# Ten gated pieces rounded by ScalarE in one go at the end of banded attention, with the step tables of the last two tiles written anew

## The reference, cut to what matters

```python
logits = einsum("bnqkgd,bnskd->bnkgqs", q, k_band) + bias      # window of 128 keys
m = maximum(max(logits), sink); p = exp(logits - m)
probs = p / (sum(p) + exp(sink - m))
o = einsum("bnkgqs,bnskd->bnqkgd", probs, v_band)
o = o.reshape(B, T, 2048) * silu(z)
x = x + o @ w_out                                              # b_w_out: 2048 x 1024
```

## Time and profile before

| | |
|---|---|
| median of 3 runs | 1502.39 us (1501.16 to 1502.45) |
| the profiled execution | 1503.07 us, of it a span of 1501.2 us |
| PE busy | 1480.6 us, 99% of the span |
| DVE, ACT, POOL busy | 926.2, 736.8, 259.7 us |
| mean granted TensorE clock | 0.998 of full speed |
| chain that ended last | PE 90%, DVE 5%, ACT 3% |

### The profile page before, as it was taken

One profiled execution on the slowest core, in us unless ns is written; L12 is line 12 of the kernel. 1 busy time (PEld: TensorE's weight loads), 2 busy tenths in 40 slices (PEclk: granted clock), 3 DMA queues, 4 the chain that ended last, 5 costly groups with the idle time before them and its releaser, 6 DMA issues.

```text
span 1501.2 us, 20571 instructions
## 1 busy us (share of the span) xinstructions
PE 1480.6 (99%) x7595; PEld 1185.0 (79%) x7595; DVE 926.2 (62%) x1740; ACT 736.8 (49%) x1292; POOL 259.7 (17%) x430
## 2 busy tenths in 40 slices
PE   9999999999999999999998999999999999999998
PEld 7878888888778878888877887665778888888887
DVE  5867777787655468788886346554475243433467
ACT  5454455644553356566675234665465241423343
POOL 1034323344302015444440000000000000000000
PEclk9999999999999999999999999999999999999999
DMA  5321111111114333232321331211223233232321
GB/s 211 99 70 61 66 58 57 57 59 55 57 57 146 108 108 103 72 91 85 92 76 59 107 97 59 64 62 42 93 90 99 88 109 99 84 103 94 98 84 70
DMA packets 40163, 127.21 MB, mean 85 GB/s; under 512 B 4576, under 2 KB 9104, under 8 KB 40064
## 3 DMA queue, kind: packets, MB, share of 16 engines
q1 hardware_dynamic: 38112, 121.65, 25.4%
q0 software_dynamic: 1040, 3.27, 0.6%
q10 hardware_dynamic: 912, 0.99, 0.2%
HBM read 122.69 MB, written 2.15 MB: 83 GB/s over the span
## 4 chain that ended last, share of the span: by engine, by line
PE 90%; DVE 5%; ACT 3%; issue 1%; DMA 0%; POOL 0%; SPq 0%; DVEq 0%; ACTq 0%; POOLq 0%
PE ps L892 88%; DVE wl L2059 1%; PE ps L1293 1%; PE ps L1037 1%; ACT wh L1440 0%; ACT sp L1955 0%; DVE up L2213 0%; DVE xr L2649 0%; DVE qkv L2097 0%; ACT sp L1953 0%; DMA wraw<-in_wa 0%; ACT xr L1720 0%; ACT L L1856 0%; ACT sp L1957 0%; DVE L L2601 0%
## 5 line engine op out<-in xcount | busy, mean ns | idle before, releaser
L892 PE MATMUL ps<-xr,wh 128*128 128x512 f32 x2720 | 875.3, 402 | 4.8 <-DVE xr L2649 3.8
L892 PEld LDWEIGHTS ps<-xr,wh 128*128 128x128 f32 x2720 | 497.9, 189 | 120.7 <-issue 25.6
L892 PE MATMUL ps<-xr,wl 128*128 128x512 f32 x1376 | 538.5, 391 | 0.0
L2059 DVE TENSOR_TENSOR wl<-wraw,wh 128x1024 fp32r<-128x1024 f32 x214 | 268.2, 1261 | 129.1 <-ACT wh L1440 128.2
L892 PEld LDWEIGHTS ps<-xr,wl 128*128 128x128 f32 x1376 | 258.7, 188 | 55.9
L1440 ACT ACTIVATE wh<-wraw 128x1024 fp32r<-128x1024 f32 x214 | 222.1, 1049 | 74.6 <-PE ps L892 73.1
L892 PE MATMUL ps<-xm,wh 128*128 128x512 f32 x640 | 197.8, 390 | 0.0
L892 PEld LDWEIGHTS ps<-xm,wh 128*128 128x128 f32 x640 | 119.5, 188 | 26.2 <-DVE xm L2735 1.6
L892 PE MATMUL ps<-xm,wl 128*128 128x512 f32 x320 | 124.5, 389 | 0.0
L2097 DVE SCALAR_TENSOR_TENSOR qkv<-cin,gains,qkv 128x512 f32<-128x512 f32 x96 | 77.8, 811 | 10.0 <-ACT qkv L1470 9.3
L1856 ACT ACTIVATE L<-L,m 128x256 f32<-128x256 f32 (+1 forms) x128 | 60.0, 472 | 31.8 <-DVE m L2607 31.8
(11 more groups left out here) (292 smaller groups left out, 1739.9 us busy)
## 6 DMA issues: line engine op xcount, KB each, us to landing
wraw<-in_wa SPq DMA_DIRECT2D x48, 512.0 KB, 3.5
wraw<-in_wb SPq DMA_DIRECT2D x32, 512.0 KB, 3.8
wraw<-in_wu SPq DMA_DIRECT2D x32, 512.0 KB, 3.4
wraw<-in_wd SPq DMA_DIRECT2D x32, 512.0 KB, 3.5
wraw<-in_wao SPq DMA_DIRECT2D x16, 512.0 KB, 3.5
wraw<-in_wbo SPq DMA_DIRECT2D x16, 512.0 KB, 3.9
wraw<-in_wc SPq DMA_DIRECT2D x16, 512.0 KB, 3.5
bias<-rel_rows SPq DMA_DIRECT2D x16, 256.0 KB, 3.8
```

Of the source, the lines that this page charges most:

```text
L892: return e.matmul(out, w, x, start=start, stop=stop, skip_group_check=True)
L2059: e.tensor_tensor(m.wl[:, i % N_SPLIT, :], m.raw[:, i % N_RAW, :], m.wh[:, i % N_SPLIT, :].bitcast(F), ALU.subtract).then_inc(s.wlo, 1)
```

## The change

Four places. ScalarE rounds pieces 4 to 13 (before: 4 to 7) in one go in `split_ob(4)`. Tile 14 carries pieces 0 to 8 (before: 0 to 7), tile 15 pieces 9 to 13 (before: 8 to 13). The tables of both tiles are new.

```diff
-    "b14": plan("x4 v0 a0 a0 x3 a0 b2 a0 b2 a0 a0 a0 a0 x8 a0"),
+    "b14": plan("x5 v0 b0 a0 a0 a0 a0 a0 x2 b2 a0 a0 a0 x8 a0"),
...
-    "b15": plan("x5 v0 x2 b2 b4 w4"),
+    "b15": plan("x5 v0 b2 b3 w5"),
...
-            g = chain(g, pieces_out("split_ob", out, 2, 0, *((0, 8) if j == 14 else (8, 14))))
+            g = chain(g, pieces_out("split_ob", out, 2, 0, *((0, 9) if j == 14 else (9, 14))))
...
-        for k in range(4, 8) if i == 4 else range(i, i) if 4 < i < 8 else (i,):
+        for k in range(4, 14) if i == 4 else range(i, i) if 4 < i < 14 else (i,):
             e.wait_ge(s.ob, k + 1)
             e.activation(m.XR[:, k, :], m.XF[:, 16 + k, :], ACT.Copy).then_inc(s.obhi, 1)
```

## The result

The changed kernel takes 1504.16 us (median of 17 runs) against 1501.29 us for the kernel before on the same chip (17 runs): ratio 1.0018, 95% interval [1.0012, 1.0025], so 2.9 us slower (1.8 to 3.8). The forecast was 1504.6 us, on a median of before that was then 1502.39 us (3 runs). One run of the filled changed kernel of experiment 5 took 2113.59 us at a mean granted clock of 0.654, and its figures leave that run out.

A forecast was written before the change was run, and what follows sets the result against it. PE was taken to bound the kernel (99% busy, 90% of the chain). New waits 1.2 + 4.4 + 1.5, less 0.46, 3.5 and 0.9, gave +2.2 us: 1504.6 us; range 1500.6 to 1507.4.

The forecast's parts named there:

- Fourteen roundings: ScalarE from 783.58: thirteen end at 790.5, the fourteenth runs 790.6 to 791.25; tile 14's first copy ends 791.76, not 790.71.
- First turn ahead of the logits: PE, in the 1.4 us query wait: logits still start at 786.64; the move takes 0.46 us off PE's path.
- Wait for the bank of `values(13)`: PE's second turn at 789.47: bank read by VectorE until 790.59, a new wait of 1.2 us.
- Split of piece 5, the step that decides: VectorE's split, behind exponentials and weight splits, ends 800.9; PE wants it at 796.6: new wait 4.4 us (3.3 to 4.9).
- What the earlier exponentials win: ScalarE: exponentials start 2.7 us earlier but end at 801.7 against 801.82, so their earlier start wins nothing.
- The bank of `values(14)`: Second turn of tile 15: PE arrives 812.9, bank free 814.45, a third wait of 1.5 us (0 to 2.5).
- The clock: Behind the wait at piece 5: granted clock falls again, costing the same 2.8 us as behind the old long wait.
- rival A: New wait at piece 5: clock does not fall, or briefly; -0.6 us, 1501.8; chance 15%.
- The sum: `values(15)` on PE begins at 817.05 against 814.83: +2.2 us, 1505.3 on the profiled execution, 1504.6 predicted.
- Rival B: Splits of pieces 5 to 8 in time, waits at pieces 5 and 8 gone: -3.4 us, 1499.0; chance 8%.

The follow-up runs named there:

- experiment 5: Changed kernel with 18 matmuls into a bank no longer read, put in PE's wait ahead of piece 5: median 1502.12 us against 1501.06 before, ratio 1.0006.
- Experiment 1: Kernel before with only the rounding changed, ScalarE rounding pieces 4 to 13 in one go: median 1501.79 us against 1501.43, ratio 1.0001.
- Experiment 3: Changed kernel with `values(13)` gated by VectorE ahead of its first five splits: median 1504.20 us against 1501.43 before, ratio 1.0015.
- Experiment 9: Changed kernel with `values(14)` gated ahead of the splits of pieces 9 to 13: median 1503.91 us against 1501.69 before, ratio 1.0016.
- Experiment 4: Changed kernel with `values(13)` gated first, then all nine splits of tile 14 ahead of the reductions: median 1503.53 us against 1501.43 before, ratio 1.0012.
- experiments 7 and 10: Two interleaved tables on the changed kernel's rounding; the second has reductions earlier and piece 4's split later: ratios 0.9965 and 0.9964, medians 1495.80 and 1495.99 us.
- experiment 8: Interleaved tables with rounding undone (pieces 4 to 7 in one go, 8 to 13 each at its own split): median 1497.91 us against 1501.06 before, ratio 0.9978.
- experiment 7: Changed kernel with interleaved tables, splits and products separate entries, VectorE's splits placed where PE needs them: median 1495.80 us against 1501.06 before, ratio 0.9965.
- filled kernel before: Kernel before with 15 matmuls into a bank no longer read, put in PE's wait ahead of piece 8: median 1500.41 us, ratio 0.9995.
- experiment 2: Changed kernel with its rounding undone (pieces 4 to 7 in one go), new tables and shares kept: median 1503.16 us against 1501.43 before, ratio 1.0008.

## Why the prediction was right

Times of the trace after are given plus 0.57, on the scale of the earlier trace rows.

- **Fourteen roundings.** Predicted from 783.58, the last from 790.6 to 791.25; measured 783.55 and 790.63 to 791.26. Experiment 1 adds that by themselves they change nothing.
- **First turn ahead of the logits.** It stands in the former wait, as predicted; the logits wait 0.86 instead of 1.42 us and start no earlier.
- **Wait for the bank of `values(13)`.** Predicted 1.2 us until 790.69; measured until 790.65, 1.01 of it shown as idle. Experiment 3 shows that little of it is paid for: without it piece 5 begins only 0.3 us earlier. In the decomposition of my sum it stood as a term of its own; the path sum, which runs through the split of piece 5, was right.
- **Split of piece 5, the step that decides.** Predicted exponentials at 795.4, split at 800.2, PE at 801.0, a wait of 4.4 us; measured 795.42, 800.16, 800.90 and 4.11. Each term of that chain (copy, mask, reductions, two exponentials, two weight blocks, mask) was a duration of the trace of before, and none changed by more than 0.1 us.
- **What the earlier exponentials win.** Nothing, as predicted: they end at 801.5, against 801.8 before, with the weight blocks between them.
- **The bank of `values(14)`.** Predicted 1.5 us, measured 1.34. Experiment 9 shows that this place too is VectorE's sum of work and not the one order: gated first, it makes piece 9 late, and only 0.3 us is won.
- **The clock.** Here the size was off. I put 2.8 us behind the new wait and took it as equal to that of before, so that it cancelled. In the profiled execution after it cost 1.65 us (5b starts at 801.13, 8b at 806.86, where six `mm3` of 0.68 make 805.21). And over many runs it does not cancel: filled, the kernel before gains 0.65 us and the changed kernel 1.8. The order alone is worth some 1.7 us where I had 2.2, the clock some 1.2 where I had 0. Neither trace is of the common kind: the execution of before that I read has a mean granted clock of 0.998, as 24 of the 74 runs of before beside the experiments have (median 1502.28), while 50 have 0.999 (1501.15); of the changed kernel the profiled one is among three runs at 0.999 (median 1503.64), and 14 lie at 0.998 or 0.997 (1504.45). My rival A, no fall at all, is what the filled kernel of experiment 5 shows: its stretch is 0.3 us shorter than in the trace of before, where A had 0.6, but against the median of before it is still 1.1 slower. No run of the changed kernel itself is under 1503.19.
- **The sum.** For the profiled execution I had 1505.3 and it was 1503.64, 1.7 less. Of this 1.0 lies in the stretch (30.4 predicted, 817.05 less 786.64, and 29.45 measured), which the clock's term, 1.15 too large, accounts for; the other 0.7 lies outside, 0.57 of it ahead of the logits. The stretch grew by 1.26 us, but the median by 2.9: the execution of before that I read (1503.07 us) lies 1.8 above the median of its 17 runs and that of after 0.5 below its own, and the two differ by 0.6, as the stretch of after began 0.57 us earlier: 1.8 + 0.6 + 0.5 is the 2.9. The forecast for the median was 0.4 us too high on a base 1.1 us too high; its step was 2.2 where 2.9 was measured. So the mechanism was right, but that the number came within 0.4 us is in part luck: a base too high and a step too small, by the clock's term, nearly cancelled.

Rival B needed the split of piece 5 in time. Experiment 4 put it there and still lost 2.1 us: VectorE's denominators and weight blocks then made piece 9 late. Only when both were spread (experiments 7 and 10) did the wait go without coming back, and in the tables of experiment 7 the early rounding paid (experiment 8: 2.1 us).

That a filled kernel before gains so little has two reasons. Its trace shows waits of 0.2 and 0.4 us in the place of the slow part, so that the stretch shrinks by 1.9 us and not by 2.8; and most of its runs have a higher mean clock than the execution that I read. How long the slow part lasts in those runs stays open, since no trace here is of one and the mean clock is given to three places only.

## What to carry to other kernels

Where two engines feed the one that bounds, moving work forward on the first gave nothing here (experiment 1) until the order on the second let it through (2.1 us, experiments 7 and 8): look, for every piece that the bounding engine asks for, at what stands ahead of it in the queue of the engine that finishes it. Removing one wait of several in a row tests which of them is paid for; here two of three were paid for by 0.3 us only. And spread such work into the idle time that the second engine has between a request and its answer, rather than ahead of or behind the whole block.

## What the runs showed of the hardware

The same wait of 4.11 us of PE was followed by 3.4 us at half clock in one execution and by at least 6.4 us in another (experiment 9); one of 2.8 us by none (experiment 2), one of 3.2 us by 4.8 us (experiment 4, from PE's restart at 809.6 to the first product at full clock, 814.4; there two waits of 1.4 and 0.25 us stand close before it). The length of the slow part is not set by the wait alone. The Trainium skill (TensorE: Matmul & The Clock Gate, Part 1: The HAM clock gate) says of the slow part at the start of a kernel that it is run-variable, because the watch on PE's activity is free-running. These traces agree for a slow part in the middle of one: 3.4 against at least 6.4 us behind the same wait. In the prediction I had this only as a reason for a rival. The 74 runs of before, with medians of 1501.15 us at a mean clock of 0.999 and 1502.28 at 0.998, show that one trace is a poor base for a difference of 2 us.

Matmuls into a bank that nobody reads, put into a known wait, kept the clock at 1.00 behind that wait in the profiled executions of both kernels that had them, and narrowed the runs of the kernel before from 2.3 us of spread (26 runs) to 0.9 (11 runs).
